# Reordering the hand-over from the merge stage to the expert stage of a hybrid diffusion kernel, and a later place for one score load

## The reference

```python
h = rmsnorm(x, norm1) * (1 + sc1) + sh1
mix = (sigmoid(ga) * y_a + sigmoid(gb) * y_b) @ w_out      # two token mixers, merged
x = x + g1 * mix
h = rmsnorm(x, norm2) * (1 + sc2) + sh2
# PEER: 8 heads, product keys, 16 experts for each head and token
q = (h @ pk_w_q).reshape(t, 8, 2, 128)
s = einsum('thpd,phkd->pthk', q, sub_keys)                 # 2 x 128 scores for each head
sv, si = top_k(s, 16)
best, pos = top_k(sv[0][..., :, None] + sv[1][..., None, :], 16)
eidx, gate = chosen si[0] * 128 + si[1], softmax(best)
act = gelu(einsum('td,thkd->thk', h, u_tab[eidx]))
out = einsum('thk,thkd->td', gate * act, v_tab[eidx])
x = x + g2 * out
y = rmsnorm(x, norm_f)
```

## Time and profile before

| what | value |
|---|---|
| median of 3 runs | 4077.87 us (4072.95 to 4086.17) |
| profiled execution, its own time | 4086.17 us |
| its span, first to last instruction | 4084.3 us |
| mean granted TensorE clock | 0.870 of full |
| busy: PE, DVE, POOL, ACT | 74%, 64%, 33%, 26% |
| first gather issued | 958.73 us |
| gathers | 1152, 1208 MB in all |

### The profile page before, as it was taken

The page is one execution under the profiler, slowest core; times in us unless marked ns, Lnnn a source line. Parts: engine busy times, 40 slices in busy tenths (PEclk is TensorE's granted clock), DMA queues, the critical chain, the costliest instruction groups (busy, mean ns, idle before and its releaser), DMA issues.

```text
span 4084.3 us, 44739 instructions
## 1 busy us (share of the span) xinstructions
PE 3031.6 (74%) x15406; PEld 1311.9 (32%) x15406; DVE 2613.3 (64%) x6282; ACT 1069.5 (26%) x2720; POOL 1343.0 (33%) x1174
## 2 busy tenths in 40 slices
PE   8999999798689999785666656665665665665555
PEld 3767767444344444221121111111111111111111
DVE  4545455666467667564787766776776776676555
ACT  2534435002123333111232222222222222221111
POOL 0000000002233444342444444444444444444443
PEclk9999999898899999897888877878878878787777
DMA  4010000557899999999999999999999999999998
GB/s 178 22 31 18 28 16 1 219 177 285 340 387 385 405 416 402 419 407 421 417 404 417 419 407 418 416 418 412 419 414 410 418 416 401 420 417 399 420 420 346
DMA packets 214316, 1346.40 MB, mean 330 GB/s; under 512 B 24738, under 2 KB 45730, under 8 KB 63170
## 3 DMA queue, kind: packets, MB, share of 16 engines
q0 software_dynamic: 165888, 1208.03, 71.9%
q1 hardware_dynamic: 48196, 135.41, 8.8%
HBM read 1329.69 MB, written 13.67 MB: 329 GB/s over the span
## 4 chain that ended last, share of the span: by engine, by line
PE 39%; DMA 38%; DVE 13%; issue 5%; ACT 3%; POOL 2%; POOLq 0%; SPq 0%; DVEq 0%; ACTq 0%
DMA arena<-in_uv,mask_b 13%; PE ps L760 13%; DMA arena<-in_uv,mask_f 10%; DMA arena<-in_uv,ones 10%; PE ps L1420 9%; DVE arena L1275 6%; PE ps L738 4%; PE ps L621 3%; DMA arena<-in_w_q 2%; POOL arena L599 2%; ACT arena L957 2%; PE ps L1464 2%; PE ps L1414 2%; PE ps L1481 1%; PE ps L680 1%
## 5 line engine op out<-in xcount | busy, mean ns | idle before, releaser
L760 PE MATMUL ps<-arena 64*64 64x512 f32 x9216 | 1451.7, 757 | 936.2 <-ACT arena L957 888.2
L1275 DVE CUSTOM_DVE_ANT_0 arena<-arena 128x1024 f32<-128x1024 f32 x1152 | 1412.6, 1226 | 954.5 <-DMA arena<-in_uv,mask_b 363.0
L760 PEld LDWEIGHTS ps<-arena 64*64 64x64 f32 x9216 | 350.7, 158 | 1906.2 <-ACT arena L957 1362.3
L957 ACT ACTIVATE arena<-arena 128x64 f32<-128x64 f32 x1152 | 338.2, 341 | 1411.5 <-DVE arena L1154 1411.5
L599 POOL DMA_INDIRECT arena<-in_uv,ones x384 | 449.3, 1170 | 659.7 <-PE ps L760 491.8
L599 POOL DMA_INDIRECT arena<-in_uv,mask_f x384 | 445.2, 1159 | 581.2 <-PE ps L760 493.6
L599 POOL DMA_INDIRECT arena<-in_uv,mask_b x384 | 442.3, 1152 | 584.9 <-PE ps L760 491.8
L1420 PE MATMUL ps<-arena 128*128 128x384 f32 x1152 | 387.9, 493 | 15.4 <-issue 13.5
L953 ACT ACTIVATE arena<-arena 128x2 f32<-128x2 f32 x576 | 117.5, 204 | 859.1 <-DVE arena L1275 858.4
L583 POOL IOTA arena<- 128x16 f32 x1 | 0.1, 145 | 889.5 <-PE ps L630 889.5
L738 PE MATMUL ps<-arena 128*128 128x384 f32 x768 | 270.3, 499 | 0.0
(11 more groups left out here) (205 smaller groups left out, 2836.1 us busy)
## 6 DMA issues: line engine op xcount, KB each, us to landing
arena<-in_w_mod SPq DMA_DIRECT2D x12, 2048.0 KB, 23.3
arena<-in_w_mg SPq DMA_DIRECT2D x16, 1536.0 KB, 21.8
arena<-in_w_in SPq DMA_DIRECT2D x28, 512.0 KB, 3.4
arena<-in_w_out SPq DMA_DIRECT2D x2, 4096.0 KB, 18.1
arena<-in_w_q SPq DMA_DIRECT2D x8, 1024.0 KB, 20.8
arena<-in_w_q SPq DMA_DIRECT2D x4, 2048.0 KB, 33.6
arena<-x_scratch SPq DMA_DIRECT2D x15, 512.0 KB, 11.3
arena<-in_uv,ones POOLq DMA_INDIRECT x384, 10.5
```

The costliest lines, as they stand in the source:

```text
L760: mm = nc.tensor.matmul(PS[c * HALF:(c + 1) * HALF, 2 * r + n, :], DG[rows, s, :], RG[s][rows, D + n * 512:D + (n + 1) * 512], start=(g == ...
L957: A(DG[:, s, :], halves, ACT.Copy, scale=COEF[:, s:s + 1]).then_inc(diag_r, 1)
L1275: ins = v.tensor_tensor_reduce(u, u, h2, 1.0, 0.0, ALU.mult, ALU.add, PRE[:, s % RING:s % RING + 1])
```

## The change

Four places change the order of instructions; no instruction is added or removed.

- SP: `score_in(1, 0)` is issued after `merge_in(0)`, `score_out(10)` and `merge_in(1)`, where it stood ahead of them.
- PE: `mix(1, 1)` is one block ahead of `turn(0)`, where it lay in three pieces around `turn(0)` and `score(0, 0)`; the first four matmuls of `mix(2, 0)` stand between these two.
- ACT: `row_norm(1)` stands ahead of `queries_out(0)`; `rows_out(1)` ahead of `gates(0, 0)`.
- DVE: both `rows_ready`, `front(0)`, `x1(1)` and `front(1)` stand ahead of all ten steps of `Pair(0, 0)`. Before, `front(0)` came ahead of the wait for `l_rows2`, and `x1(1)`, the second `rows_ready` and `front(1)` stood between its third and fourth steps.

```diff
@@ SP
-        score_in(1, 0)
         sp.wait_ge(q_r, len(QUERY_ORDER))
         merge_in(0)
         score_out(10)
         sp.wait_ge(sc_r, len(QUERY_ORDER))
         merge_in(1)
+        score_in(1, 0)
         score_out(11)
@@ PE
         queries_early(0, 0)
         queries_early(0, 1)
-        mix(1, 1, range(2))
+        mix(1, 1)
         turn(0)
-        mix(1, 1, range(2, 4))
+        mix(2, 0, range(4))
         score(0, 0)
-        mix(1, 1, range(4, KD))
-        mix(2, 0)
+        mix(2, 0, range(4, KD))
         mix(2, 1)
@@ ACT
         rows_out(0)
+        row_norm(1)
         queries_out(0)
         turned_out(0)
         scores_out(0)
-        row_norm(1)
+        rows_out(1)
         gates(0, 0)
-        rows_out(1)
@@ DVE
         rows_ready(W2A[0], N2A)
-        front(0)
-        dve.wait_ge(x1_a[0], 16)
-        dve.wait_ge(it_r, 1)
-        first = Pair(0, 0).steps()
-        for step in first[:3]:
-            step()
-        x1(1)
         dve.wait_ge(l_rows2, 32)
         rows_ready(W2A[1], N2A)
+        front(0)
+        x1(1)
         front(1)
-        dve.wait_ge(x1_a[1], 16)
-        for step in first[3:]:
+        for t in range(2):
+            dve.wait_ge(x1_a[t], 16)
+        dve.wait_ge(it_r, 1)
+        for step in Pair(0, 0).steps():
             step()
```

## The result

The changed kernel takes 4107.6 us in the median of 4 runs (4100.5 to 4111.72), the kernel before 4076.74 in the median of the 4 beside it. The ratio is 1.0072, with a 95% interval from 1.0052 to 1.0091: slower by 0.7%, some 29 us (30.9 between the medians). Forecast were 4099 us, 21 us slower. The profiled execution took 4109.35 us, its span is 4107.0 us.

The account below looks back on a forecast made before the run. The expert stage was taken as held by gathers (DMA share 0.9 or more after 1000 us). Late start 11.4 us plus late score read 9.9 us made 21.3 us on the median 4077.9: forecast 4099 us, range 4086 to 4112.

Parts of the forecast that it names:

- The wait for the latent rows: At the start, DVE waits for l_rows2's second load, landing at 924.15, so front(0) begins 7.8 us late.
- mix(1, 1) and mix(2, 0) ahead of the scores: On PE before Pair(0, 0)'s scores: all of mix(1, 1) takes 3.5 us, four matmuls of mix(2, 0) 1.7.
- The clock: PE at 1.2 GHz after idling: 0.9 us in the transposes, 0.7 in the queries, 2.2 in turn, mix(2, 0) and scores.
- The start term: Lateness of the first gather: 7.6 + 0.9 + 0.7 + 2.2 = 11.4 us, bounds 7.6 and 13.1.
- the pair in one piece: DVE's ten steps of Pair(0, 0) run uninterrupted, taking 16.0 us instead of 22.9, which gives back 6.9 us.
- The score read: Pair(1, 0)'s read behind merge_in(1) lands at 1225.5; DVE stalls 18 to 19 us; net term 9.9 us, bounds 6 and 14.
- The stall of ACT for the store: Before gathers at 1233.70, ACT's wait until 1226.20 for the last score's store is swallowed; the place costs 10.5 us, not 18.
- the two paces: The score read's landing behind merge_in(1): 1224.8 if its rest goes alone at 410 GB/s, 1226.1 at the store's pace.
- The likeliest case: Late start and late score read both cost near their forecast sizes: 4099 us, chance 0.66.
- both stalls are worse: Rival: after DVE's stall, late merge blocks run at 1.2 GHz for some groups, 10 us more, 4109; chance 0.15.
- only the start: Rival: Pair(1, 0)'s read is hidden and only the start is late, 4089.3 us, 4085.5 with high clock; chance 0.12.
- the start costs nothing: Rival: l_rows2 lands by 916.3 and the start is about 0 late, only the read costs, 4088 us; chance 0.04.

Follow-up runs that it names:

- sp_only: The kernel before with only SP's score_in(1, 0) moved behind merge_in(1); ratio 1.0024 to the kernel before, 10 us slower.
- start_only: The changed kernel with SP's order put back as before; ratio 1.0046 to the kernel before, 19 us slower.
- gap_filled: The changed kernel with PE's mix(1, 1) moved ahead of front(0); ratio 1.0026 to the kernel before, start 47.6 us.
- rows_back: The changed kernel with front(0) and x1(1) ahead of DVE's wait for l_rows2; ratio 1.0030 to the kernel before, start 53.0 us.
- again_before: The kernel before, unchanged, measured again for a second profile and the spread; single executions 4074.59 to 4094.41 us.
- again_after: The changed kernel, unchanged, measured again for a second profile; ratio 1.0068 to the kernel before.

## Why the prediction was right, and where its sizes were off

**What bounds the kernel.** Right at both places: in the two profiles of the changed kernel 20.2 and 17.9 us of lag, counted from the start of x1(0), are left at the last gather, and the two halves add up in the time. But the page was misread. Its digits are 9 only from 1123 us on; the slice from 1021 to 1123 has 8, and so has the last. In that slice and just behind it PE waits for query weights, and there the first profile of the changed kernel gave back its 6 us. A lag can shrink there, and single profiles drift later too: sp_only's lag grows from -0.3 us at slot 88 to 5.9 at the last gather, start_only's from 6.0 to 9.6.

**The wait for the latent rows.** Right: predicted 7.8 us, measured 7.1 (front(0) comes 12.4 us after the start of x1(0) instead of 5.3). Two rows of the trace before, an issue and a landing, gave it.

**mix(1, 1) and mix(2, 0) ahead of the scores.** The step that failed is the sentence "four matmuls are one of the 1.88 us blocks, with overlap some 1.75, eight are 3.5". The x4 of that row counts instructions, and each matmul call of this program shows as two of them (a transpose as one): that block was `range(2)`. So mix(1, 1) is x16 and took 7.03 us, not 3.5, and the four of mix(2, 0) are x8, 3.6 us at the full clock (gap_filled), not 1.7. That is 5.4 us of the start. The row of the first projections, in the trace before, would have told: three halves of eight steps stand there as x48.

```profile
898.32 20.84 PE L648 MATMUL ps<-arena 128*128 128x512 f32 x48 [1.48 <-DVE arena L1003]
```

**The clock.** The mechanism was right, with 0.9 us in the transposes as forecast. The queries cost 2.5 us more, where 0.7 was taken and 0 to 2 allowed (9.10 to 9.63 us in the five profiles that have this gap); turn and mix(2, 0) cost 2.2 more (1.12 and 5.36 against 0.66 and 3.60 in gap_filled; 1.7 in the three other profiles with the gap of 4.57 us) where 2.2 was taken for these and the scores, which took 1.05 as before. rows_back and gap_filled show that this is the gap's doing: without it the queries take 7.14 us there, and in six of the seven other profiles without it. The seventh, again_before, is an exception that the account doesn't cover. PE had idled only 1.28 us ahead of the transposes and 1.27 ahead of the queries, and still the granted clock fell (PE's timeline and a window of 2 us):

```profile
922.40 8.61 PE L680 MATMUL ps<-arena 128*128 128x256 f32 x32 [1.27 <-ACT arena L838]
...
922.00:924.00 2.00, 1.60 (x4) 1.36 (x5) 0.00 (x0) 0.26 (x1) 0.00 (x0) 0.50 1.03 367
```

These 1.5 us are the whole difference between the starts of the two profiles of the kernel before, 46.4 and 47.9. So the clock can cost 1.5 us in the queries in the kernel before too; why it did in one profile is open.

**The start term.** Predicted 11.4 us with bounds of 7.6 and 13.1; measured 17.5 in the first profile and 14.7 to 16.5 between the others, so outside its bounds each time. The 16.0 us for the pair in one piece held (16.1), so what was given back was right too.

**The score read.** Right in mechanism and size. The read landed at 1236.1; the 1225.5 of the sum plus the 10.8 us by which slot 80 was late is 1236.3. DVE's stall was forecast at 17 to 19 us and measured 17.7; the place at 10.5, and measured 10.1 from slot 80 to 88. The 0.6 us for the read that no longer runs at 1160 would lie ahead of slot 80, where profiles differ by 2 to 3 us, and can't be told there. The stall of ACT for the store was swallowed, as said: slot 86 comes 11 us after slot 82, not 18 as in the kernel before, so the net is not the stall's 18 us.

One part of the way there was different. The sum let the load land at 1222.9 and the read follow at its own pace, 2.6 us behind. With the lag taken off, the load landed at 1224.7 and the read 0.6 us behind it, at 1225.3. The store that was issued 3.6 us behind that load had landed 3.2 behind it; the read was issued 0.6 us behind. The end of both together fits, the pace of the read alone was not seen.

So the 1224.8 and the 1226.1 of the two paces weighed can't be told apart by this landing. The Trainium skill (DMA: Bandwidth & Descriptors, Queues, rings and completion order) says that each DMA engine takes turns, packet by packet, between the queues it has work for. This landing does not contradict what the prediction drew from that rule, a lone read with the engines to itself, but does not show it either.

**The sum.** 21.3 us predicted, 29 measured (28 in again_after). Of the difference 5.4 us are the blocks of mix taken at half their length and 1.8 the clock in the queries. The likeliest case was the one that happened, with one term too small. The time, 4107.6, fell inside the range, in its upper fifth, nearer to the 4109 of "both stalls are worse" than to the 4099 of the forecast, and it is partly luck that it did: the range had that room for another reason, a run of late merge blocks at 1.2 GHz. That did not happen: the merge blocks behind the stall (line 738, from 1242.81) took 3.5 us each, as before. The rivals "only the start" and "the start costs nothing" are excluded by sp_only and start_only.

Of the signs named for the profile after, two failed, both by the start term: the first MAX8 came at 959.71, not at 950 to 954, and the first gather at 976.12, not at 966 to 972.

## What to carry to other kernels

When work is moved on one engine to run in one piece, ask what the other engines do in that time: the same orders of DVE and ACT came with a start longer by 17.5 or by 1.2 us here, by where one 7 us block of PE stood. A small transfer behind a large load on one queue landed just after the load here (the read 0.6 us, the store 3.2 us behind it); give a read its place by when it is needed, not by when it could first be issued, and the same holds for a small store that someone waits for. Count a block's instructions in the profile against the loop in the code before scaling its time.

## What the runs showed of the hardware

PE's longest two waits for query weights in the first tile were 11 to 14 us or 4.3 to 6.1 us long (8.3 and 9.3 in one run each), in runs whose instructions there are the same. The second of the pair of loads behind them landed 38.8 to 45.8 us after its issue. Two profiles of one kernel can therefore differ by some 7 us at that place (slots 48 to 50 took 13.9 and 21.3 us in those of the changed kernel), more than half of the smaller of the two effects studied; the two distances compared here, on either side of it, agree to within 2.4 us. Why a load draws one or the other was not tried.
